# The in1 operand of the gathered-row dots: normalized rows in SBUF instead of a PSUM copy

## The reference

```
qb = (xb @ w_q).reshape(TOKEN_BLOCK, PEER_HEADS, 2, PEER_DKEY)
s = einsum('thcd,hcnd->thcn', qb, sub_keys)
...                                   # top 16 x top 16, best 16 of them: eidx, g = softmax(best)
ug = take(u, eidx, axis=0)            # 8 heads * 16 rows of 1024 for each token
vg = take(v, eidx, axis=0)
h = gelu(einsum('td,thkd->thk', xb, ug))
out = einsum('thk,thkd->td', g * h, vg)
x = layer_norm(ALPHA * x + out, ln2_g, ln2_b)
```

## Time and profile before

| | |
|---|---|
| median of 3 runs | 1775.45 us (1773.05 to 1778.77) |
| the profiled execution | 1774.55 us, its span 1772.4 us |
| granted PE clock, mean | 0.983 |
| PE / PEld busy | 96% / 84% |
| DVE busy | 71% |
| ACT / POOL busy | 36% / 34% |
| stages, us from the span's start | attention, projections and first norm to about 506; queries and top-k from there; u part to about 1190; v part to about 1745; second norm to the end |
| matmuls of u tiles and projections (L1156 to L1158, 1440 each) | 516.2, 509.4 and 508.9 us |
| matmuls of v tiles (768 each) | 305.9, 304.3 and 304.2 us |
| dots, L1052 (128) | 150.8 us, 1216 ns each |
| DMA, 16 engines, whole span | 239 GB/s |

### The profile page before, as it was taken

The page is one execution under the profiler, slowest core; times in us unless marked ns, Lnnn a source line. Parts: engine busy times, 40 slices in busy tenths (PEclk is TensorE's granted clock), DMA queues, the critical chain, the costliest instruction groups (busy, mean ns, idle before and its releaser), DMA issues.

```text
span 1772.4 us, 23346 instructions
## 1 busy us (share of the span) xinstructions
PE 1700.3 (96%) x8969; PEld 1492.6 (84%) x8969; DVE 1262.4 (71%) x2325; ACT 639.2 (36%) x1011; POOL 605.3 (34%) x270
## 2 busy tenths in 40 slices
PE   8999998899979999999999999997999999999997
PEld 6898896677768899999999999996777777778775
DVE  1003345555259995998899999957888898888886
ACT  3213333443232234334344435432333343333333
POOL 4423221225353463444344433432232232322202
PEclk9999999999989999999999999998999999999999
DMA  5422101112312267777798999999999999999981
GB/s 190 172 81 72 48 24 50 48 60 83 143 48 96 84 179 276 240 246 280 255 335 323 333 345 335 348 365 376 373 376 372 380 376 377 367 382 379 385 278 60
DMA packets 144382, 422.76 MB, mean 239 GB/s; under 512 B 11152, under 2 KB 76944, under 8 KB 123024
## 3 DMA queue, kind: packets, MB, share of 16 engines
q1 hardware_dynamic: 125840, 287.05, 45.3%
q0 software_dynamic: 18432, 134.23, 20.2%
HBM read 368.80 MB, written 52.43 MB: 238 GB/s over the span
## 4 chain that ended last, share of the span: by engine, by line
PE 62%; DVE 24%; DMA 10%; issue 2%; ACT 1%; POOL 1%; SPq 0%; POOLq 0%; ACTq 0%; DVEq 0%
PE bank L1156 18%; PE bank L1157 18%; PE bank L1158 18%; DMA raw<-in_uv 7%; DVE acc L1066 6%; DVE wlo L1044 6%; DVE uvb L1052 4%; PE bank L1377 2%; DVE alo L1096 2%; DVE af L1089 2%; PE bank L1245 1%; PE bank L1212 1%; PE xpair L1260 1%; DMA gl<-g_scratch 1%; PE bank L1214 1%
## 5 line engine op out<-in xcount | busy, mean ns | idle before, releaser
L1156 PE MATMUL bank<-xhi,whi 128*128 128x384 f32 (+1 forms) x1440 | 516.2, 358 | 12.1 <-DVE xlo L796 8.5
L1157 PE MATMUL bank<-xlo,whi 128*128 128x384 f32 (+1 forms) x1440 | 509.4, 354 | 0.0
L1158 PE MATMUL bank<-xhi,wlo 128*128 128x384 f32 (+1 forms) x1440 | 508.9, 353 | 0.0
L539 POOL DMA_INDIRECT uvb<-in_uv,eidx x128 | 214.0, 1672 | 391.2 <-DVE acc L1066 371.0
L709 ACT ACTIVATE whi<-raw 128x1024 fp32r<-128x1024 f32 x256 | 270.0, 1055 | 207.6 <-DMA raw<-in_uv 135.4
L1156 PE MATMUL bank<-whi,ahi 128*128 128x512 f32 x768 | 305.9, 398 | 20.4 <-DVE alo L1096 20.4
L1157 PE MATMUL bank<-wlo,ahi 128*128 128x512 f32 x768 | 304.3, 396 | 0.0
L1158 PE MATMUL bank<-whi,alo 128*128 128x512 f32 x768 | 304.2, 396 | 0.0
L1156 PEld LDWEIGHTS bank<-xhi,whi 128*128 128x128 f32 x1440 | 273.5, 190 | 30.3 <-issue 12.0
L495 POOL TENSOR_TENSOR wlo<-raw,whi 128x2048 fp32r<-128x2048 f32 (+1 forms) x38 | 170.0, 4475 | 358.2 <-ACT whi L569 358.1
L1158 PEld LDWEIGHTS bank<-xhi,wlo 128*128 128x128 f32 x1440 | 273.2, 190 | 17.8
(11 more groups left out here) (191 smaller groups left out, 1870.6 us busy)
## 6 DMA issues: line engine op xcount, KB each, us to landing
raw<-in_u SPq DMA_DIRECT2D x128, 512.0 KB, 6.0
raw<-in_uv SPq DMA_DIRECT2D x128, 512.0 KB, 8.9
h_scratch<-hout SPq DMA_DIRECT2D x128, 192.0 KB, 6.3
g_scratch<-stage SPq DMA_DIRECT2D x48, 512.0 KB, 7.9
hl<-h_scratch SPq DMA_DIRECT2D x32, 768.0 KB, 10.3
gl<-g_scratch SPq DMA_DIRECT2D x32, 768.0 KB, 12.3
raw<-in_w_in SPq DMA_DIRECT2D x22, 1024.0 KB, 4.8
raw<-in_w_q SPq DMA_DIRECT2D x8, 1024.0 KB, 4.7
```

The source lines that it names most:

```text
L539: nc.gpsimd.indirect_dma_start(out=uvb[:, k % UVB, :], out_offset=None, in_=a["uv"][:, :], in_offset=bass.IndirectOffsetOnAxis(ap=eidx[:, ...
L1156: mm(out, lh, rh, start=first, stop=False)
L1157: mm(out, lh, rl, start=False, stop=False)
L1158: return mm(out, ll, rh, start=False, stop=last)
```

## The change

in1 of the dots becomes `xn[:, 0, :]`, the two copies of ACT go, with ACT's wait for `xt_lo` ahead of them, and DVE's wait for the copies goes. The banks stay allocated. The number, order and size of all other instructions is the same.

```diff
-        x_copied, idx_done = sem("x_copied"), sem("idx_done")
+        idx_done = sem("idx_done")
...
                 nc.scalar.activation(qT[:, n % 2, :], bank[n % 2][:, :], ACT.Copy).then_inc(q_out, 1)
-                if n == 0:
-                    act.wait_ge(xt_lo, 2 * TC)
-                    for j in range(2):
-                        nc.scalar.activation(xpair[:, j * S:(j + 1) * S], xn[:, 0, j * S:(j + 1) * S], ACT.Copy).then_inc(x_copied, 1)
                 if n % 2 == 1:
...
                     u = uvb[:, k % UVB, 0:D]
-                    V.tensor_tensor_reduce(out=u, in0=u, in1=xpair[:, :], scale=1.0, scalar=0.0, op0=ALU.mult,
+                    V.tensor_tensor_reduce(out=u, in0=u, in1=xn[:, 0, :], scale=1.0, scalar=0.0, op0=ALU.mult,
                                            op1=ALU.add, accum_out=hd[:, k:k + 1]).then_inc(dot_done, 1)
...
             V.scalar_tensor_tensor(eidx[:, :], picks[:, 0, 0, :], float(P), picks[:, 1, 0, :], ALU.mult, ALU.add).then_inc(idx_done, 1)
-            dve.wait_ge(x_copied, 2)
             for beat in range(POOL_ONLY // 2, NT):
```

## The result

The changed kernel is slower: 1785.68 us (median of 16 runs, 1779.62 to 1792.36) against 1775.09 us (1770.45 to 1783.01), ratio 1.0057 with a 95% interval of 1.0041 to 1.0073, about 10 us. The range forecast ended at 1781.5. The profiled execution has a span of 1780.8 us, 8.4 us over that of before.

A forecast was written before the change was run, and what follows sets the result against it. PE was taken to bound the u part, and PE, DVE and the DMA engines together the v part. 1774.55 + 0 + 0 + 0.2 + 0 = 1774.75 us profiled, forecast 1775.7 us, range 1771 to 1781.5.

The forecast's parts named there:

- Parts 1 and 2: ACT's two copies (1.11 us from 519.18) and DVE's wait for them go; each was forecast at 0.
- Part 3: The dot with an SBUF operand: +3 ns on 1216 ns, hidden in the u part, +0.2 us in the v part.
- Part 4: Dots against POOL's subtractions in the u part: three pairs blocked, 6.6 us on DVE, 0 on PE.
- The bank path: At beat 27, a blocked dot delays ACT's bank-freeing GELU about 2.3 us; 0.9 us left, so 0 on PE.
- A: Slower: blocked dots of the u part reach PE through ACT's late GELU; 6.6 us, 1782.3 us; chance 0.11.
- B: A little slower: dots cost what L1066 costs; +2.1 us, +5.5 at most, 1777.6 to 1781.0; chance 0.08.
- C: Faster: PE's 10.8 us of waits for `alo` in the v part shrink; all gone 1764.9 us; chance 0.04.
- C's half: Half of PE's 10.8 us of waits for `alo` in the v part gone: 1770.3 us.

The follow-up runs named there:

- pairs 5 and 7: Against the kernel before, only the dot pairs of beats 26 and 30 read `xn` in SBUF; 1773.98 us, ratio 1.0004.
- `delay_pair_1`: Against the kernel before, all dots still read PSUM, but DVE does two unused extra dots ahead of the pair of beat 15; 1780.05 us, ratio 1.0028.
- `pairs_1_3`: Against the kernel before, only the dot pairs of beats 15 and 21 read `xn` in SBUF; 1783.46 us, ratio 1.0046.

## Why the prediction was wrong

**Parts 1 and 2 (copies and wait, 0): right.** Keeping them changes nothing that can be measured. In the changed kernel ACT waits for PE 4.85 us ahead of the second evacuation, where 4.95 was said.

**Part 3 (the dot +3 ns): right.** The median went from 1216 to 1218 ns, and within one kernel (the v part in SBUF) it is 1221 against 1217 ns with PSUM; that kernel, with 80 SBUF dots in the v part, is at 0.9993.

**Part 4, which dots are blocked: right for the undisturbed timing.** The pairs at 732.59, 824.46 and 858.09 were named, and putting just those back in PSUM removes the whole loss. (The text gave the pair at 824.46 to beat 27; it is beat 26.) In the changed kernel itself the blocked ones are the first, the last and the pair of beat 21, since by then everything had moved. 2.2 us for one block was right as well.

**Part 4, what a blocked dot costs: the step that failed.** The prediction set "6.6 us, all between 732 and 863" against "11.6 us of waits for ACT and 6.2 us for PE" from the earlier trace rows and wrote 0 for PE. Three things were wrong in that.
- It took the other DVE instructions as fixed. Behind the first block four groups of them with two SBUF inputs slid under POOL subtractions; 2.2 us grew to 10.4 gross. The added delay with PSUM dots shows that these need no blocked dot.
- It compared sums over 182 us and gave a place only for the 6.2 us. What counted was the slack on the spot: 2.7 us of waits between 738 and 766, and 5.5 us by which the subtraction of 766.43 was ahead of PE. One block fits into that, a cascade of 7.9 us net does not. For pairs 5 and 7 the same sum came out right, as the waits there (4.7 and 6.2 us) lie directly behind and the following instructions missed POOL.
- It checked PE's price only through ACT and the bank. The path through DVE's own `wlo`, which carried 8.3 of the 9.1 us, was not followed at all. The bank path was sized well: it gave way from 3.2 us of lateness on by the text (2.3 us and the 0.9 us left). In the changed kernel the pair of beat 26 came about 4.0 us late relative to PE, and PE paid 0.8 us. (The 4.0 is an estimate. The first dot of the pair is at 835.57. The 824.46 of before, less 1.1 us for the earlier start, plus the 8.3 us that PE had lost itself, is 831.6.)

Left out too was the clock: the two stops lost 1.5 and 1.7 us at the lower clock, not in any term.

**The rivals.** A had the right sign and, as one of two conditions, "shifted DVE work brings new overlaps"; its path (ACT and the bank) carried 0.8 us of 9.1, and its price of 6.6 us was too low. A's sum should have been run forward through the next beats. B is refuted by the dots of the v part, 1221 ns and not 1285, and C by that kernel's time: PE's waits for `alo` are 10.0 us there against 10.8, and the interval from 0.9974 leaves out C's half, 5.4 us (0.9970). The range, said to take in half of C, began at 1771 and C's half lay at 1770.3; nothing hangs on that here.

What stays open: why the clock falls at one stop and not at another, and why the timed ratio of one stop alone (1.0015, interval 0.9995 to 1.0034) lies below the 4.1 us of its trace (1.0023). The interval covers both. A stop without the fall costs 2.7 us, which would be 1.0015, but whether the clock fell in the executions that were only timed is not shown.

## What to carry to other kernels

Where two engines exclude each other, a delay is not worth its own length. Shift the rest of the queue by it and look for new overlaps, beat by beat, up to the first wait that takes the delay in; then compare with the slack of every product that the late engine owes, not only with that of the nearest one. Before an operand moves into SBUF, look not at its price (here 2 to 4 ns) but at which neighbours on POOL it will exclude, near misses included. If there are few such places, an order between the two engines there can cost nothing, as it did here (1.0003).

## What the runs showed of the hardware

- When POOL's subtraction begins during a DVE instruction with two SBUF inputs and another such instruction follows at once, POOL goes next and the second waits for all of it: 3.4 us for a dot of 1.22. This was so for each of the 16 blocked dots in seven kernels.
- A small instruction is blocked as long as a large one: `jf`, 128 columns, went from 0.29 to 2.16 us.
- Two inputs are not needed in every case. In the kernel before, a cast with one SBUF input took 2.50 us where 0.29 is usual, behind a subtraction of POOL that began 0.13 us ahead of it, at 774.75:

```profile
774.88 2.50 DVE L981 CAST idf<-idx 128x256 bf16<-128x256 uint32 x1
```

- PE's stops of 2.4 us did not all bring the clock down. It fell to 0.50 for 3.4 us at 8 of the 10 stops in the traces of six kernels; in `delay_pair_1` and at the first stop of `pairs_1_3` it stayed at 1.00. Such a stop cost 2.7 us, those with the fall 4.0 to 4.2 us in the changed kernel.
